# A gated recurrence on one core: the order of work on five engines, and who multiplies the tree of decays

## What is computed

```python
def chunk_scan(q, k, v, logf, s0):
    """S_t = diag(f_t) S_{t-1} + k_t v_t^T, o_t = S_t^T q_t, chunkwise."""
...
    def step(S, inp):
        qb, kb, vb, gb = inp
        G = jnp.cumsum(gb, axis=1)
        o_inter = jnp.einsum('bthk,bhkv->bthv', qb * jnp.exp(G), S)
        decay = jnp.exp(jnp.where(earlier_or_same, G[:, :, None] - G[:, None, :], -jnp.inf))
        A = jnp.einsum('bthk,bshk,btshk->bhts', qb, kb, decay)
        o_intra = jnp.einsum('bhts,bshv->bthv', A, vb)
        G_last = G[:, -1]
        S_new = jnp.exp(G_last)[..., None] * S + jnp.einsum('bshk,bshv->bhkv', kb * jnp.exp(G_last[:, None] - G), vb)
        return S_new, o_inter + o_intra
...
    oc_f, S_f = chunk_scan(qc, kfc, vc, gfc, s0)
    oc_b, S_b = chunk_scan(flip(qc), flip(kbc), flip(vc), flip(gbc), s0)
    ol_f, _ = chunk_scan(ql, kfl, vl, gfl, S_f)
    ol_b, _ = chunk_scan(flip(ql), flip(kbl), flip(vl), flip(gbl), S_b)
```

## Time and profile before

| | us |
|---|---|
| median of three runs | 3906.14 |
| least and most of them | 3900.93, 3912.29 |
| the profiled execution | 3909.69 |
| its span | 3907.7 |
| stage of the recurrence, in the span | 807.6 to 1053.6 |
| TensorE busy, of the span | 3560.9 (91%) |
| VectorE busy | 2585.6 (66%) |
| ScalarE busy | 1877.3 (48%) |
| GpSimd busy | 790.5 (20%) |
| granted TensorE clock, mean | 0.954 |

### The profile page before, as it was taken

How to read it: one execution, slowest core, us unless ns; L and a number is a source line. 1 busy time by engine, 2 the same in 40 slices (tenths; PEclk the granted TensorE clock), 3 DMA queues, 4 the chain that set the end, 5 groups by cost and what they waited for, 6 DMA issues and landing times. The chain is left out here.

```text
span 3907.7 us, 43104 instructions
## 1 busy us (share of the span) xinstructions
PE 3560.9 (91%) x16760; PEld 2846.0 (73%) x16760; DVE 2585.6 (66%) x2881; ACT 1877.3 (48%) x2428; POOL 790.5 (20%) x624
## 2 busy tenths in 40 slices
PE   7999889964697999999999998999898989999989
PEld 4887744664685888888878786788776678787857
DVE  6546266876767888889888887556575545516753
ACT  5211111355463777767777776342464323515731
POOL 2100025500021110111111114210243223203422
PEclk9999989977897999999999999999998999999999
DMA  5554314220236999999999996365411433525133
GB/s 198 201 186 143 124 43 172 84 110 19 94 139 228 379 366 382 378 366 379 376 372 370 362 379 200 107 208 178 168 54 56 164 109 110 165 103 186 48 102 119
DMA packets 322788, 774.50 MB, mean 198 GB/s; under 512 B 26072, under 2 KB 110419, under 8 KB 322328
## 3 DMA queue, kind: packets, MB, share of 16 engines
q1 hardware_dynamic: 299802, 694.94, 48.9%
q0 software_dynamic: 17856, 66.33, 5.2%
q10 hardware_dynamic: 4928, 10.49, 0.8%
HBM read 660.21 MB, written 111.48 MB: 197 GB/s over the span
## 5 line engine op out<-in xcount | busy, mean ns | idle before, releaser
L3398 DVE TENSOR_TENSOR first_expert_w_low<-shared_z,first_expert_w_high 128x2048 fp32r<-128x2048 f32 x127 | 297.1, 2380 | 80.0 <-ACT first_expert_w_high L3351 79.5
L3398 DVE TENSOR_TENSOR moe_w_low<-moe_w_raw,moe_w_high 128x2048 fp32r<-128x2048 f32 x128 | 287.3, 2285 | 52.6 <-ACT moe_w_high L3351 52.1
L3398 DVE TENSOR_TENSOR moe_w_low<-shared_z,moe_w_high 128x2048 fp32r<-128x2048 f32 x128 | 290.5, 2310 | 19.9 <-ACT moe_w_high L3351 19.9
L3351 ACT ACTIVATE first_expert_w_high<-shared_z 128x2048 fp32r<-128x2048 f32 x126 | 234.9, 1918 | 121.0 <-DMA shared_z<-in_exp_w 118.4
L3351 ACT ACTIVATE moe_w_high<-moe_w_raw 128x2048 fp32r<-128x2048 f32 x128 | 238.3, 1911 | 91.2 <-DMA moe_w_raw<-in_exp_w 83.9
L3626 POOL TENSOR_SCALAR layer_att_p<-layer_att_p,layer_att_rinv,layer_att_neg_lam 128x1280 f32<-128x1280 f32 (+1 forms) x72 | 173.4, 2408 | 529.9 <-DVE layer_att_neg_lam L3655 314.2
L3351 ACT ACTIVATE moe_w_high<-shared_z 128x2048 fp32r<-128x2048 f32 x128 | 238.5, 1915 | 54.1 <-DMA shared_z<-in_exp_w 48.3
L177 PE MATMUL moe_bank<-moe_w_high,first_expert_xgT_high 128*128 128x512 f32 x640 | 252.7, 395 | 0.0
L3633 DVE TENSOR_REDUCE layer_att_nb<-layer_att_scores 128x1 f32<-128x1280 f32 (+1 forms) x144 | 195.0, 1369 | 86.4 <-PE layer_att_scores L3538 85.4
L178 PE MATMUL moe_bank<-moe_w_low,first_expert_xgT_high 128*128 128x512 f32 x640 | 250.8, 392 | 0.0
L179 PE MATMUL moe_bank<-moe_w_high,first_expert_xgT_low 128*128 128x512 f32 x640 | 250.6, 391 | 0.0
(11 more groups left out here) (660 smaller groups left out, 9522.1 us busy)
## 6 DMA issues: line engine op xcount, KB each, us to landing
shared_z<-in_exp_w SPq DMA_DIRECT2D x128, 2048.0 KB, 10.1
moe_w_raw<-in_exp_w SPq DMA_DIRECT2D x64, 2048.0 KB, 9.9
shared_z<-in_w_in SPq DMA_DIRECT2D x48, 512.0 KB, 6.2
first_raw<-in_w_in SPq DMA_DIRECT2D x32, 512.0 KB, 7.3
front_vec<-in_ada_w POOLq DMA_DIRECT2D x16, 1024.0 KB, 6.0
proj_t<-front_out SPq DMA_DIRECT2D x48, 256.0 KB, 2.0
shared_z<-in_w_mod SPq DMA_DIRECT2D x24, 512.0 KB, 4.5
k_high<-layer_front_staged SPq DMA_DIRECT2D x20, 512.0 KB
```

Source lines behind the costliest of these rows:

```text
L3351: nc.scalar.activation(hi, x, ACT.Copy).then_inc(high, 1)
L3398: nc.vector.tensor_tensor(lo, x, hi.bitcast(F32), ALU.subtract).then_inc(low, 1)
```

## The change

The order of five queues is changed, and the doublings move from VectorE to GpSimd. On SP, mask and v are issued first. On ScalarE, `queries` of the next head stand at level 1, `sigmoids` at 2 and 4, `gates` at 3 and 5. On TensorE `turn` stands ahead of `state`. On VectorE `carry_state(h - 1, k)` stands at level k + 1, one earlier. In the tail the outputs of head 2 stand ahead of the first `turn` of head 3, the second `turn` waits for two selects fewer, and two `o_copy` stand earlier. GpSimd waits by semaphore for the gates or the level before, and for VectorE's last reading of what it overwrites in `tree`.

```diff
--- before.py
+++ after.py
@@ -2317,10 +2317,10 @@
                     sp.dma_start(core.hg_o[half * UT * P:(half + 1) * UT * P, h * P:(h + 1) * P].rearrange("(t p) c -> p t c", p=P),
                                  ob[u % 2].rearrange("p (t c) -> p t c", c=P)).then_inc(core.hstore[u % 2].sem, 16)
 
+                sp.dma_start(mask[:, :, :], io["t_pair_masks"][:, 0:LEVELS * P].rearrange("p (i t) -> p i t", t=P)).then_inc(masks, 16)
+                sp.dma_start(v[:, :, :], core.vg[:, 0:BANK].rearrange("(t p) c -> p t c", p=P)).then_inc(inputs, 16)
                 load_q(1)
                 load_z(1)
-                sp.dma_start(mask[:, :, :], io["t_pair_masks"][:, 0:LEVELS * P].rearrange("p (i t) -> p i t", t=P)).then_inc(masks, 16)
-                sp.dma_start(v[:, :, :], core.vg[:, 0:BANK].rearrange("(t p) c -> p t c", p=P)).then_inc(inputs, 16)
                 for h in range(1, H):
                     if h + 1 < H:
                         load_q(h + 1)
@@ -2342,6 +2342,25 @@
                     last = nc.gpsimd.memset(to[:, TOK + SEQ:2 * TOK], 0.0)
                 last.then_inc(zeroed, 1)
 
+                def double(h, j):
+
+                    if j:
+                        pool.wait_ge(totals, LEVELS * h + j)
+                    elif h:
+                        pool.wait_ge(gated, h)
+                    if h and j < LEVELS - 1:
+                        pool.wait_ge(ahead, LEVELS * (h - 1) + j + 2)
+                        pool.wait_ge(behind, LEVELS * (h - 1) + j + 2)
+                    elif h:
+                        pool.wait_ge(sdone, 2 * STEPS * h)
+                    (tile, at), (to, to_at), n = total(j), total(j + 1), TOK >> (j + 1)
+                    nc.gpsimd.tensor_tensor(view(to, to_at, [[1, 3 * n]]), view(tile, at, [[2, 3 * n]]),
+                                            view(tile, at + 1, [[2, 3 * n]]), ALU.mult).then_inc(totals, 1)
+
+                for h in range(H):
+                    for j in range(LEVELS):
+                        double(h, j)
+
             @block.scalar
             def _(act):
                 def sigmoids(h, d):
@@ -2427,19 +2446,19 @@
                             kt_copy(h - 1, j)
                         if h >= 2 and j in (1, 2):
                             o_copy(2 * (h - 2) + j - 1)
-                        if more and j in (3, 4):
-                            gates(h + 1, j - 3)
-                        if more and j in (2, 3):
+                        if more and j in (3, 5):
+                            gates(h + 1, j // 2 - 1)
+                        if more and j in (2, 4):
                             if (h, j) == (0, 2):
                                 act.wait_ge(zeroed, 1)
-                            sigmoids(h + 1, j - 2)
-                        if more and j == 5:
+                            sigmoids(h + 1, j // 2 - 1)
+                        if more and j == 1:
                             queries(h + 1)
                 first_gate()
                 for k in range(NSB):
                     kt_copy(H - 1, k)
-                    if k in (2, 4):
-                        o_copy(2 * (H - 2) + k // 4)
+                    if k in (1, 2):
+                        o_copy(2 * (H - 2) + k - 1)
                 o_copy(2 * H - 2)
                 first_squares()
                 o_copy(2 * H - 1)
@@ -2486,7 +2505,7 @@
                         pe.wait_ge(behind, LEVELS * (h + 1))
                         pe.wait_ge(placed, LEVELS * (h + 1))
                     if h == H - 1 and k == 1:
-                        pe.wait_ge(masked, 2 * LEVELS * H)
+                        pe.wait_ge(masked, 2 * LEVELS * H - 2)
                     elif n:
                         pe.wait_ge(kts, n - 1 if h == H - 1 and k else n)
                     for j, s in enumerate(batch(k)):
@@ -2531,18 +2550,18 @@
                     for j in range(LEVELS):
                         for half in range(2):
                             level(h, half, j)
+                        if h and j < NSB:
+                            turn(h - 1, j)
                         if h and 1 <= j <= NSB:
                             state(h - 1, j - 1)
-                        if h and j < NSB:
-                            turn(h - 1, j)
                         for p in (2 * j, 2 * j + 1):
                             if h >= 2 and p < PAIRS:
                                 out(h - 2, p)
+                for p in range(PAIRS):
+                    out(H - 2, p)
                 turn(H - 1, 0)
                 turn(H - 1, 1)
                 for k in range(NSB):
-                    if k < PAIRS:
-                        out(H - 2, k)
                     state(H - 1, k)
                     if k + 2 < NSB:
                         turn(H - 1, k + 2)
@@ -2568,6 +2587,7 @@
                         dve.wait_ge(placed, n)
                         dve.wait_ge(ahead, n)
                         dve.wait_ge(totals, n)
+                        dve.wait_ge(behind, n)
                         dve.wait_ge(prod, 2 * n)
                     elif h:
                         dve.wait_ge(begun, h)
@@ -2592,12 +2612,6 @@
                                                        ALU.mult)
                     last.then_inc(behind, 1)
 
-                def double(h, j):
-
-                    (tile, at), (to, to_at), n = total(j), total(j + 1), TOK >> (j + 1)
-                    nc.vector.tensor_tensor(view(to, to_at, [[1, 3 * n]]), view(tile, at, [[2, 3 * n]]),
-                                            view(tile, at + 1, [[2, 3 * n]]), ALU.mult).then_inc(totals, 1)
-
                 def select(h, half, j):
                     m = 16 * h + 2 + 2 * j + half
                     n = 2 * (LEVELS * h + j) + half
@@ -2614,6 +2628,8 @@
                     n = h * NSB + k
                     if h >= 2 and k == 0:
                         dve.wait_ge(odone, PAIRS * (h - 1))
+                    if k == 0:
+                        dve.wait_ge(totals, LEVELS * (h + 1))
                     dve.wait_ge(ds, n + 1)
                     for j, s in enumerate(batch(k)):
                         d, i = divmod(s, STEPS)
@@ -2631,9 +2647,8 @@
                     for j in range(LEVELS):
                         outer(h, j)
                         inner(h, j)
-                        if h and j >= 2:
-                            carry_state(h - 1, j - 2)
-                        double(h, j)
+                        if h and 1 <= j <= NSB:
+                            carry_state(h - 1, j - 1)
                         if j == 0 and h == 0:
                             dve.wait_ge(masks, 16)
                         if j == LEVELS - 1 and h + 1 < H:
```

## The result

The changed kernel takes 3862.69 us (median of four runs, 3859.28 to 3871.49) against 3907.84 for the one before (3900.93 to 3912.29): a ratio of 0.9889, with an interval of 0.9867 to 0.9912. The forecast was 3876.5, the range 3848 to 3896. The gain is 45.2 us where 29.6 were forecast.

The account below looks back on a forecast made before the run. The stage was taken as bound by a chain of waits round the engines, no engine full. Terms +4.4, -14.3, -9.5, -3.8 (heads 0 to 3) and -6.4 (tail) gave -29.6 us: 3876.5 for the median, range 3848 to 3896.

Parts of the forecast that it names:

- The ring: Heads 1 and 2: VectorE waits for ScalarE, transpose, state product, then VectorE again; 18.9 and 18.0 us idle.
- no `kt_copy` would wait over 3 us: ScalarE, heads 0 to 2: sign that copies find their transposes done; one had waited 8.27 us before.
- The reorder, head by head: Heads 1 and 2: new order leaves VectorE 0.5 and 4.5 us of waits; with GpSimd's turns 50.6 and 54.7 us.
- 4.5 us of waiting: Head 2: VectorE waits 2.1 us for state behind out's products, and 2.4 with ScalarE's two o_copy and queries.
- The SP queue: Head 0: mask and v first removes the mask wait; q of head 1 lands about 819, queries end about 823.
- GpSimd's price: Doublings on GpSimd at a step of one's price: 4.35 us for 1920 elements, 9.5 us a head.
- The turns in head 0: Level 6 and begin: inner's halves and begin each wait for one GpSimd doubling, 8.95 us; turns cost head 0 10.4.
- Head 3 and the tail: Head 3 up to its last inner 40.4 against 44.2 us, -3.8; last outputs 6.4 us sooner after it.
- 1 (no turns): GpSimd's reads don't hold VectorE up and the tree is hidden; gain 56.6 us, 3849.5; chance 0.10.
- 2: GpSimd pays for the step of two; at 1.74 times, 27 us, 3903; chance 0.09 for a price of 1.4 to 1.8.
- 3: Heads 0 to 2, GpSimd price from 1.8 on: slower, 3923 at 2.3 times; chance 0.05 over +0.3%, 0.03 just under.
- 4: TensorE's granted clock stays at its lower level through out and state; head 2 and tail lose 12 us, 3889; chance 0.13.

Follow-up runs that it names:

- e5: The kernel before with one edit: turn of the head before issued ahead of state on TensorE; 3872.13 us in one run, against 3907.91 before.
- e1: The changed kernel with the doublings given back to VectorE, behind the carries, so the new order alone; 3856.61 us, ratio 0.9865.
- e7: The changed kernel with other operands for GpSimd's first doubling in heads 2 and 3 and a 30-element product ahead in head 1; 3857.41 us in one run.
- e9: The changed kernel with the old tail: head 2's outputs between head 3's states, the old wait and the two o_copy back; 3866.01 us in one run.
- e10: The order alone, tree on VectorE, plus 16 unneeded GpSimd products of 512 elements from the gates of heads 1 and 2; heads 0 to 2 153.8 us against 132.8.
- e4: The changed kernel with GpSimd's doublings in heads 1 to 3 held back to VectorE's carries and selects, the first cut in three; 3853.27 us, ratio 0.9856.
- e11: The order alone, tree on VectorE, plus 18 unneeded GpSimd settings of 1152 elements to a constant; heads 0 to 2 133.2 us against 132.8.
- e12: The order alone, tree on VectorE, plus 24 unneeded GpSimd copies of 512 elements; heads 0 to 2 142.2 us against 132.8.
- e3: The changed kernel with each doubling made twice by GpSimd, into the same place; 3879.92 us in one run.
- e6: The changed kernel with the old SP order, load_q(1) and load_z(1) ahead of mask and v; 3870.16 us in one run.
- e2: The kernel before with only the doublings moved to GpSimd, with their waits; 3916.34 us, ratio 1.0013.

## Why the prediction was right, and where it was not

**What bounds the kernel.** Right. The ring was there and the exchange of `turn` and `state` opened it: e5 alone takes heads 1 and 2 from 129.2 to 102.2. Of the sign that no `kt_copy` would wait over 3 us, one fails: in head 3 one waits 3.39 for TensorE (970.97). It costs VectorE nothing, whose one wait in that head is earlier (2.24, at 966.16).

**The reorder, head by head.** The terms that the sum names add up to 50.4 for head 1 and 54.4 for head 2, not to 50.6 and 54.7; half a microsecond in all. The steps were laid out well where VectorE's own work decides: with the tree on VectorE (4.46 us) the prediction's terms give 46.6 for head 1, and e1 shows 46.0. For head 2 they give 50.6, and e1 shows 46.0, without any wait: its 4.5 us of waiting were put down to `state` behind `out`. They do occur in the changed kernel (4.1, among them 2.29 at 914.86), because there VectorE reaches its first carry of head 2 some 2.0 us earlier (it is ready 10.4 us after the end of `begin`; in e1 the carry starts 12.3 after it), by the doubling that it no longer does. So the step was right for the kernel it was made for, and it also says that part of what GpSimd takes off VectorE comes back as waiting.

**The SP queue.** Order and mask together were to bring 6.0 in head 0; e1 shows 6.7. The landing of q was forecast at 819 and the end of the queries at 823; they are 822.6 and 824.8, the stage itself starting 2.6 later than before. The wait that this left (`inner` at levels 3 and 4 behind ScalarE, 0.51 and 1.35) was forecast as 1.5.

**GpSimd's price.** Mis-sized: 4.35 for the 1920 elements measured 3.39, and the six others 1.79 down to 0.23, some 7.7 a head in place of 9.5. I had written that below a step of one's price I saw no reason to go; e7 shows that it is lower all the same, and not why. In head 2 the turns cost 5.3 where 8.3 were forecast: 2.31 at `outer` for 3.45, which is the price, and 3.0 for 4.9 at `inner` and `begin`. Of that the price is some 0.6; the rest is mostly that each turn costs VectorE 0.2 less than the GpSimd instruction's length.

**The turns in head 0.** This is the step that failed: 8.95 us at level 6 and `begin` of head 0 were forecast, and nothing was lost there. The gates ended when they should, GpSimd started its doubling at 843.85, 0.05 us behind `outer` of level 6, and then stood until `begin` had ended at 850.5. The prediction had read "one whole instruction each" out of the earlier trace rows, where VectorE came second. Part of it was paid later: the doubling ran beside the two selects and into `outer` of the next level 0 (4.50 for 2.57), and the two behind it held `inner` (5.03 for 2.65), 4.3 together. That is why head 1 has an excess of 9.8 and not 5.5. It came out at 51.6 for a forecast of 50.6 by two errors against each other, so that this agreement is luck: the price too high, and a tree that reaches into its level 0 not foreseen.

**Head 3 and the tail.** -4.1 for -3.8, and -5.9 for -6.4; by e9 the new tail is worth 5.9 of it by itself.

Together, by head: -7.1, -13.4, -12.8, -4.1 and -5.9 are -43.3, where +4.4, -14.3, -9.5, -3.8 and -6.4 were -29.6. Head 0 holds 11.5 of the difference of 13.7: the 8.95 that weren't lost at level 6 and `begin`, 0.7 of the order (e1), and some 1.9 at its early levels, which I did not take apart.

**The rivals.** 1 (no turns) is refused by the rows at 889.80 and by e10. 2 and 3 fall with the price of 3.39. 4: the granted clock rose in each stretch (0.71, 0.76, 0.83, 0.94 against those of the earlier trace rows), and the eight products of a `state` took 1.75 us in head 1 (868.36) and 1.13 in the tail (1000.69), for 2.04. A rival that I had not put: that the change as a whole is right and its part on GpSimd is not. The prediction's own terms say so, though it did not add them up: +10.4 in head 0, 8.3 for 4.46 in heads 1 and 2 and 4.46 saved in head 3 make the move 13.6 us dearer, where 8.0 were measured. The tree on VectorE costs 17.8 us; on GpSimd it costs 19.8 of excess and 5.0 more of waiting (8.5 for 3.4), which is 7.0 of the 8.0 us by which the heads are longer than in e1; the tail is 1.3 shorter. On the whole program that is 6 us (3862.69 for 3856.61), with intervals that touch; the trace carries this verdict, not the medians. It turns round only where the doublings are placed beside reads of PSUM (e4, 170.9 for 175.5).

**What stays open.** Who gets in when both want to read. The Trainium skill, page "SBUF — State Buffer", section "Who interferes with whom", has a VectorE instruction with two SBUF inputs contend with a GpSimd one that reads, and not with one that only writes; the traces agree (e10 +21.0, e11 +0.5 us). It leaves the whole instruction to whoever issues first, and that agrees as well where one is clearly first (889.08 before 889.80); but it doesn't say who is next. Where GpSimd was at work first the two mostly alternated, though a doubling of e4 that shows 0.04 us ahead of an `outer` (941.91) was kept out until 947.0. Where it came while VectorE was at work, it got in at the next instruction in some cases (813.13, 0.46 us behind; in e10 one at 869.74, 0.07 behind) and in others only when VectorE came to read PSUM (843.85, 0.05 behind; 853.78 in e10, 0.04 behind; 840.60 in e7, 0.10 behind). How close it came doesn't decide it: of 30 GpSimd instructions that came 0.02 to 0.12 us behind a VectorE row, in all runs, 14 were kept out over two further rows or more and 16 got in at the next, among these a copy of e12 that came 0.03 behind (881.52). The place repeats: at `outer` of level 6 of head 0 all six that came 0.05 to 0.12 behind were kept out until `begin` had ended (in the changed kernel, e3, e4, e6, e7 and e9), and the one of e2, 0.19 behind, got in at the next row. I did not settle it.

## What to carry to other kernels

When no engine is full, look for the ring of waits and for the one place where a producer's instruction stands behind another that waits for the ring's end; here exchanging two calls on one queue brought 29.9 of the 45.4 us that the whole new order takes off the heads (e5, e1). Work moved to GpSimd that reads SBUF is not off VectorE while VectorE reads two operands from SBUF: it costs VectorE nearly its GpSimd length, not its VectorE length, unless it is placed beside VectorE's reads of PSUM. A step's worth should be asked for the kernel it ends up in, since a faster engine arrives earlier at the next wait.

## What was unexpected of the hardware

- A GpSimd product of neighbouring elements (step of two, 1920 elements) takes 3.39 us, that of two contiguous halves 4.24.
- A GpSimd instruction can be kept from reading over a whole row of VectorE instructions: 3.39 us became 10.02, and 0.24 became 6.84.
- A GpSimd copy of 512 elements (0.61 us), which reads one place, takes turns with VectorE as a product does; 38 us of settings to a constant cost VectorE nothing.
